# Contributions in 64x64 tiles of the array, factors per 32 tokens and a copy on ScalarE, in the recurrence of a hybrid encoder layer

## What is computed

```python
b = jnp.cumsum(log_f, axis=3)
b_mid, b_last = b[:, :, :, C // 2 - 1:C // 2, :], b[:, :, :, C - 1:, :]
scores = einsum('bhntd,bhnsd->bhnts', q * exp(b - b_mid), k * exp(b_mid - b))
scores = where(lower, scores, 0.0)
o_intra = einsum('bhnts,bhnse->bhnte', scores, v)
contrib = einsum('bhnsd,bhnse->bhnde', k * exp(b_last - b), v)
decay = exp(b_last)
# over the chunks: state_in -> decay * state_in + contrib
o_inter = einsum('bhntd,bhnde->bhnte', q * exp(b), states_in)
o = o_intra + o_inter          # forward direction + flipped direction, then RMSNorm and a gate
```

## Time and profile before

| | |
|---|---|
| median of 3 runs (lowest, highest) | 1155.76 us (1155.71, 1155.80) |
| the profiled execution, its time | 1155.74 us |
| its span, first to last instruction | 1154.0 us |
| TensorE busy | 1142.4 us, 99% |
| VectorE, ScalarE, GpSimd busy | 54%, 40%, 8% |
| recurrence, 594 to 697 us | 9% of the span |

### The profile page before, as it was taken

The page is one execution under the profiler, slowest core; times in us unless marked ns, Lnnn a source line. Parts: engine busy times, 40 slices in busy tenths (PEclk is TensorE's granted clock), DMA queues, the critical chain, the costliest instruction groups (busy, mean ns, idle before and its releaser), DMA issues.

```text
span 1154.0 us, 16043 instructions
## 1 busy us (share of the span) xinstructions
PE 1142.4 (99%) x6071; PEld 922.4 (80%) x6071; DVE 623.4 (54%) x776; ACT 462.5 (40%) x682; POOL 92.6 (8%) x82
## 2 busy tenths in 40 slices
PE   9999999999999999999999999999999999999997
PEld 7888888888888777666788788888888888888886
DVE  6755555553333685444588966655455555542223
ACT  6423223232222445554767755534423223232223
POOL 0000000000001120000055420020000000000000
PEclk9999999999999999999999999999999999999999
DMA  6332232232323331111131122423232232232221
GB/s 205 110 109 93 89 109 91 98 127 99 101 86 135 128 125 63 65 55 56 55 111 39 56 75 92 164 92 110 92 109 91 91 109 83 98 101 101 91 91 73
DMA packets 31679, 111.59 MB, mean 97 GB/s; under 512 B 3984, under 2 KB 5136, under 8 KB 31376
## 3 DMA queue, kind: packets, MB, share of 16 engines
q1 hardware_dynamic: 30192, 104.11, 26.5%
q10 hardware_dynamic: 1440, 6.82, 1.6%
HBM read 105.41 MB, written 4.19 MB: 95 GB/s over the span
## 4 chain that ended last, share of the span: by engine, by line
PE 95%; DVE 2%; ACT 2%; DMA 1%; issue 1%; ACTq 0%; DVEq 0%
PE ps L1157 26%; PE ps L1158 26%; PE ps L1159 26%; PE ps L1193 3%; PE ps L1191 3%; PE ps L1192 3%; PE ps L1297 1%; PE ps L1308 1%; PE ps L1323 1%; DMA raw<-up_dram 1%; PE ps L1452 0%; PE ps L1428 0%; PE ps L1357 0%; DVE w_lo L762 0%; PE ps L1182 0%
## 5 line engine op out<-in xcount | busy, mean ns | idle before, releaser
L1157 PE MATMUL ps<-h_hi,w_hi 128*128 128x512 f32 x1024 | 407.3, 398 | 0.2 <-DVE w_lo L762 0.2
L1159 PE MATMUL ps<-h_hi,w_lo 128*128 128x512 f32 x1024 | 398.9, 390 | 0.0
L1158 PE MATMUL ps<-h_lo,w_hi 128*128 128x512 f32 x1024 | 398.9, 390 | 0.0
L762 DVE TENSOR_TENSOR w_lo<-raw,w_hi 128x1024 fp32r<-128x1024 f32 (+2 forms) x190 | 235.3, 1241 | 193.4 <-ACT w_hi L408 187.6
L408 ACT ACTIVATE w_hi<-raw 128x1024 fp32r<-128x1024 f32 (+1 forms) x182 | 196.0, 1080 | 172.1 <-PE ps L1159 96.1
L1157 PEld LDWEIGHTS ps<-h_hi,w_hi 128*128 128x128 f32 x1024 | 192.2, 188 | 55.9 <-issue 15.6
L1158 PEld LDWEIGHTS ps<-h_lo,w_hi 128*128 128x128 f32 x1024 | 192.3, 188 | 41.3 <-issue 2.9
L1159 PEld LDWEIGHTS ps<-h_hi,w_lo 128*128 128x128 f32 x1024 | 192.2, 188 | 40.6
L478 ACT ACTIVATE g_hi<-un 128x512 f32 (+1 forms) x44 | 27.8, 632 | 250.8 <-DVE un L762 250.8
L762 DVE TENSOR_TENSOR un<-ps,rs 128x512 f32<-128x512 f32 x44 | 30.4, 691 | 122.2 <-PE ps L1159 122.2
L1157 PE MATMUL ps<-g_hi,w_hi 128*128 128x512 f32 x176 | 68.5, 389 | 0.0
(11 more groups left out here) (243 smaller groups left out, 1206.8 us busy)
## 6 DMA issues: line engine op xcount, KB each, us to landing
raw<-up_dram SPq DMA_DIRECT2D x86, 512.0 KB, 3.2
raw<-proj_dram SPq DMA_DIRECT2D x26, 512.0 KB, 3.2
raw<-down_dram SPq DMA_DIRECT2D x16, 704.0 KB, 4.1
raw<-down_dram SPq DMA_DIRECT2D x22, 512.0 KB, 3.2
raw<-gates_dram SPq DMA_DIRECT2D x16, 512.0 KB, 3.2
raw<-branch_dram SPq DMA_DIRECT2D x8, 512.0 KB, 3.2
raw<-wout_dram SPq DMA_DIRECT2D x8, 512.0 KB, 3.4
x_spill_dram<-xT ACTq DMA_DIRECT2D x1, 2048.0 KB, 7.0
```

Source lines behind the costliest of these rows:

```text
L762: return V.tensor_tensor(out, a, b, op)
L1157: T.matmul(ps[:, bank, :], w_hi[:, slot, cols], moving_hi(j), start=start and j == 0, stop=False)
L1158: T.matmul(ps[:, bank, :], w_hi[:, slot, cols], moving_lo(j), start=False, stop=False)
L1159: ins = T.matmul(ps[:, bank, :], w_lo[:, slot, cols], moving_hi(j), start=False, stop=stop and j == tiles - 1)
```

## The change

- The keys are copied once, for all 128 partitions (`k_nat`, `keys_to_sbuf`), without zeros. `contributions` takes 64 rows of them and of v for a stretch of 64 tokens, so each product is a 64x64 tile of the array; its row half is the token half, its column half the head. They write banks 6 and 7 (even and odd stretches).
- ScalarE copies them from there to `con_sb` in the order of the scan (`contributions_to_sbuf`, new), at the head of its round for tile u. `scan_states` reads `con_sb`. The mean matmul, the key transposes (now bank 7) and `norm_mean` get their banks when that copy is done (`ccp_done`).
- Factors per 32 tokens: GpSimd takes four differences per stretch (`spans`), ScalarE the exponentials `far_q`, `growth` and `edge` of 8, 32 and 16 elements. `k_end` is now the finished `k_sc` times `growth`, `q_pad` the finished `q_sc` times `edge`; the full exponentials of k_end and b_cum and GpSimd's full subtraction are not there any more. `log_f` no longer waits for k_end.
- VectorE does `query_key` ahead of `mask_scores` in odd tiles, and `yb_lo` behind the scan and the w_lo split.
- The outputs use banks 4 and 5, and the carried products go in the order 0, 2, 1, 3, 4, 6, 5, 7, so that neighbours are in different column halves.

```diff
@@ GpSimd
-            def to_end(u):
+            def spans(u):
                 pool.wait_ge(b_done, u + 1)
...
-                nc.gpsimd.tensor_tensor(supers(k_end[:]), end.unsqueeze(2).to_broadcast([P, NSUP, SUPER]), b3,
-                                        ALU.subtract).then_inc(d3_done, 1)
...
+                nc.gpsimd.tensor_tensor(span[:, u % 2, :, :, :].rearrange("p e n m -> p n e m"), ends.unsqueeze(3).to_broadcast(shape),
+                                        mids.unsqueeze(2).to_broadcast(shape), ALU.subtract).then_inc(fd_done, 1)
             def key_to_end(u):
-                pool.wait_ge(e3_done, u + 1)
-                pool.wait_ge(k_done, u + 1)
-                nc.gpsimd.tensor_tensor(k_end[:], k_end[:], k_in[u % 2][:], ALU.mult).then_inc(ke_done, 1)
+                pool.wait_ge(ks_done, u + 1)
+                pool.wait_ge(fac_done, u + 1)
...
+                nc.gpsimd.tensor_tensor(by_chunk(k_end[:]), by_chunk(k_sc[u % 2][:]),
+                                        growth[:, u % 2, 1 - u % 2, :, :].rearrange("p n m -> p (n m)").unsqueeze(2)
+                                        .to_broadcast([P, 2 * NSUP, CHUNK]), ALU.mult).then_inc(ke_done, 1)
@@ ScalarE
-                A(fac[:, u % 2, :, :], fac[:, u % 2, :, :], ACT.Exp).then_inc(fac_done, 1)
+                d, b3 = u % 2, b[:].rearrange("p (n c) -> p n c", c=SUPER)
+                A(far_q[:, d, :], span[:, d, d, :, 1 - d], ACT.Exp, scale=-1.0)
+                A(growth[:, d, :, :, :], span[:, d, :, :, :], ACT.Exp).then_inc(fac_done, 1)
+                A(edge[:, d, :, :], b3[:, :, 16:49:32] if d else b3[:, :, 15:48:32], ACT.Exp).then_inc(edge_done, 1)
...
-                act.wait_ge(d3_done, u + 1)
-                A(k_end[:], k_end[:], ACT.Exp).then_inc(e3_done, 1)
...
-                A(b[:], b[:], ACT.Exp).then_inc(e4_done, 1)
...
-                for b, tokens in enumerate(head_rows):
-                    A(k_nat[b][tokens, :, :].rearrange("p j c -> p (j c)"), ps[tokens, 6, :], ACT.Copy).then_inc(kn_done, 1)
+                A(k_nat[:].rearrange("p j c -> p (j c)"), ps[:, 7, :], ACT.Copy).then_inc(kn_done, 1)
+            def contributions_to_sbuf(u):
+                act.wait_ge(con_done, u + 1)
+                if u:
+                    act.wait_ge(state_done, u)
+                A(con_sb[:].rearrange("p (e j b) -> p b j e", j=ST, b=2),
+                  ps[:, 6:8, 0:S // 2].rearrange("p b (j e) -> p b j e", e=HD), ACT.Copy).then_inc(ccp_done, 1)
...
             for u in range(TILES):
+                contributions_to_sbuf(u)
                 if u and u % 2 == 0:
                     norm_mean(u // 2 - 1)
@@ VectorE
             def query_from_edge(u):
-                dve.wait_ge(e4_done, u + 1)
+                dve.wait_ge(edge_done, u + 1)
+                dve.wait_ge(qs_done, u + 1)
...
-                    tt(q_pad[u % 2][rows, a, :], b_cum[u % 2][rows, :], hq[rows, u // 2, :], ALU.mult).then_inc(qe_done, 1)
+                    tt(chunks(q_pad[u % 2][rows, a, :]), chunks(q_sc[rows, :]),
+                       edge[rows, u % 2, :, :].rearrange("p n m -> p (n m)").unsqueeze(2).to_broadcast([HD, 2 * NSUP, CHUNK]),
+                       ALU.mult).then_inc(qe_done, 1)
...
             def scan_states(u):
-                dve.wait_ge(con_done, u + 1)
+                dve.wait_ge(ccp_done, u + 1)
...
-                con, flat = ps[:, 4, :], state[u % 2][:].rearrange("p e n -> p (e n)")
+                con, flat = con_sb[:], state[u % 2][:].rearrange("p e n -> p (e n)")
@@ TensorE
             def mean_square(t):
                 pe.wait_ge(osq_done, t + 1)
-                pe.wait_ge(kn_done, 2 * min(2 * t + 3, TILES))
+                pe.wait_ge(ccp_done, min(2 * t + 3, TILES))
...
             def contributions(u):
-                pe.wait_ge(kn_done, 2 * u + 2)
+                pe.wait_ge(kn_done, u + 1)
...
-                        ins = T.matmul(ps[rows, 4, :].rearrange("p (e n) -> p e n", n=NSUP)[:, :, n],
-                                       k_nat[n % 2][:, j, HD * a:HD * (a + 1)], v_h[:, j, HD * h:HD * (h + 1)], start=True, stop=True)
+                        ins = T.matmul(ps[rows, 6 + n % 2, HD * j:HD * (j + 1)],
+                                       k_nat[tokens, j, HD * a:HD * (a + 1)], v_h[tokens, j, HD * h:HD * (h + 1)], start=True, stop=True)
...
-                for n in range(NSUP):
+                for n in (0, 2, 1, 3, 4, 6, 5, 7):
```

70 lines of the change are left out of this document (34 added, 36 removed).

## The result

| | before | after |
|---|---|---|
| median (lowest, highest), 6 executions each on one chip | 1155.78 us (1155.56, 1155.99) | 1159.80 us (1158.50, 1160.68) |
| ratio, 95% interval | | 1.0034 [1.0024, 1.0044] |
| the profiled execution, its span | 1155.74, 1154.0 us | 1159.83, 1158.0 us |
| busy over the same work (594 to 697 us before, 594 to 701 us after): TensorE, VectorE, ScalarE, GpSimd | 99.89, 83.55, 71.36, 43.55 us | 100.30, 80.97, 67.72, 37.38 us |

What follows compares the result with a forecast made beforehand. TensorE bounds the recurrence, ScalarE and VectorE close behind. Shifts of -1.1 (tiles 0, 1), -0.25 with mean +1.6 (2, 3), +1.0 (4, 5) and +1.25 (6, 7) were summed to +0.9: 1155.74 + 0.9 = 1156.6 us, range 1154.2 to 1158.6.

Steps and rivals of the forecast that it cites:

- the copy at 0.60: ScalarE's new copy of the contributions out of PSUM to con_sb: 0.60 us taken, 0.53 to 1.17 kept as bounds.
- +0.9: Sum of TensorE's forecast shifts over all eight tiles, in us against the kernel before.
- rival 2: ScalarE's contributions copy takes 1.17, adding 0.57 us ahead of each of three mean matmuls: 1158.3 us; chance 0.10.
- Rival 4: TensorE's clock falls to 1.2 GHz in a 1.6 us wait, 2.7 us more, three times: 1164 us; chance 0.05.
- the waits for k_end of 0.4 and 0.6: Key transposes on TensorE wait for GpSimd's k_end: 0.4 us in tiles 2 and 3, 0.6 at tile 6's transposes.
- Tiles 0 and 1: TensorE's first pair: the 0.29 wait goes and contributions save 0.45 and 0.35, together -1.1 us.
- the carried turns: Seven carried products on TensorE take four turns in either order: nothing gained; at best -2.4 us over eight tiles.
- The chain of 5.26: ScalarE's work from the o_t copies to the mean matmul takes 5.26 us, so TensorE waits 1.6 in tiles 2, 4, 6.
- rival 1: VectorE's state scan is not held beside GpSimd's k_end: sum -0.35, 1155.4 us; chance 0.22.
- The old wait for the state: TensorE's wait of 1.00 us before tile 3's outputs, for the state scan, was forecast to go.
- Rival 3: Four contribution tiles don't run at once, as both column halves write one bank; 2.05 us lost: 1158.7 us; chance 0.05.
- rival 5: ScalarE comes in time, the mean matmul doesn't wait, the 3.1 us ceiling shows: 1152.7 us; chance 0.08.

Runs made afterwards that it cites:

- The flat copy: Changed kernel with contributions 16 bytes apart in PSUM, so ScalarE's copy reads with jumps and writes con_sb without gaps: 1157.70 us, ratio 1.0014.
- the run with the filled waits: Changed kernel with 16 unused products of 256 columns on TensorE ahead of each of three mean matmuls: 1158.17 us, ratio 1.0020.

## Why the prediction was wrong

**The step that failed first: the copy at 0.60.** I took the row of the same size and source, though I had named the other bound, 1.17, from decay's row, and said that no row had such writes. It measured 1.14, so the row that I had set aside was the nearer one. That is 0.54 us on ScalarE, three times ahead of the mean matmul, 1.6 us: from +0.9 to +2.5, or 1158.3, rival 2 to the tenth. The flat copy shows it from the other side. The Trainium skill (SBUF — State Buffer, Door 1: The DMA port swizzle) has each access that crosses to a new 16-byte line pay a penalty, which spoke for the upper end. The runs agree with it, 0.58 against 1.14, though with one distance between writes they can't tell this rule from another price of writes that jump.

**The second: the clock.** Rival 4 had 0.05, since the clock was 1.00 through waits of 1.04. The wait became 2.23 because the first step was off, and behind two of three such waits the clock fell. Its price was mis-sized the other way: 2.7 us each on TensorE in the rival, 1.66 in the trace (5.29 against 3.63), and 1.6 to 2.3 us for both at the end, by the run with the filled waits. (Three times 2.7 on the forecast is 1164.7, not the rival's 1164.) Nothing in the profile of before had a wait of that length, so the size of the wait, not the row, should have moved this chance.

**Place by place.** The forecast's shift at the end of each pair of tiles was -1.35 (outputs of tile 3), -0.35 (of tile 5) and +0.9; the trace has +0.09, +2.24 and +4.04. The misses of 1.4, 1.2 and 0.5 a pair hold the copy's 0.54 each time. In the first two pairs they also hold what a fall cost, less the waits for k_end of 0.4 and 0.6 that I had forecast and that did not come.

**The sum mended.** +0.9, +1.6 and +2.3 make 4.8. The forecast also held waits of 0.4 and 0.6 for k_end; after, and in the run with the filled waits too, TensorE is so late that they are covered. That gives 3.8, and the mark says 4.04. By the medians more stays unexplained: without falls the change costs 1158.17 - 1155.8 = 2.4 us, where 0.9 + 1.6 - 1.0 gives 1.5. Some 0.9 us of the 4.0 then has no place in the sum.

**What held.** Tiles 0 and 1: -1.25 by the key transposes of tile 2, of which -0.12 stood before tile 0's contributions, so -1.13; forecast was -1.1. The contributions take 0.69 for 32 passes, the small exponentials are 0.10 to 0.12 apart, and the carried turns gain nothing. The mean matmul waits for con_sb in tiles 2, 4 and 6, and the savings ahead of it are lost in it. The chain of 5.26 from the o_t copies to the mean: measured 619.96 - 614.19 = 5.77, longer by 0.51, which is the copy's 0.54. The scan is held (1.60 in the median, against 1.21 with one operand in PSUM), so rival 1 falls. The Trainium skill's rule (SBUF — State Buffer, two separate sides), by which a VectorE instruction with two SBUF inputs and a GpSimd instruction that reads SBUF exclude each other, agrees with it: up to 2.07 in later runs, where the scan starts just behind k_end. The old wait for the state is gone. Rival 3 is refuted, the four tiles run at once. Of rival 5, a mean that doesn't wait, the price is not right: taken away, the wait came back at the key transposes, 2.21 us, and in place of the 1152.7 that the sum of TensorE's list promised the kernel took 1157.2, or 1154.7 with the clock up.

**Two sizes that did no harm here.** I took k_end at 1.05, and it is 1.23 to 1.29. I held that the spans on GpSimd would cost far less than 1.04 if they weren't covered; they take 0.80 for 32 elements, and only the gap of 4 us and more ahead of them made them free.

**What stays open.** What decides whether the clock falls behind a given wait. In the profiled executions it fell behind 11 of the 12 waits of 2.12 to 2.33 us, behind both of 3.06 and 3.30, and not behind 1.73, 1.80 or 2.06. It also fell behind 1.52 and 1.48 with a second wait of 0.75 behind them, and behind 1.20 with 0.76, but not behind 1.12 with 0.75. Other executions of the same kernels show a clock of 0.999, so length alone doesn't decide. What a fall costs at the end also differs from kernel to kernel: two go with 1.1 us in the kernel with the mean moved, 1.6 to 2.3 in the changed kernel, 2.5 with the mean in its own banks and 3.0 with the keys copied first. The wait of 3.30 for con_sb in the run with k_sc ahead of the norm's last product was not priced apart.

## What to carry to other kernels

When a step has two possible prices and both end in the same queue, look at what the higher one does to the wait behind it before choosing: here 0.54 us more turned a wait that left the clock alone (1.73) into one behind which it fell in two of three places (2.23). Where three engines are nearly full, a shorter list on the first is worth only what the others can follow, so follow the freed time to the next wait on each of them; the moves that let ScalarE, VectorE and GpSimd follow brought 3.2 us (1157.17 to 1153.96), more than the edit itself. A change of two parts is best priced apart: one half gained 1.0 us, the other lost 5.0. And where single executions spread by 2 us and more, look at the clock of each before comparing medians: two medians can differ by how often the clock fell.
